# Gate products of the second up stage in the rounded format: the product split in a high and a low part, its low rows made on VectorE and ScalarE

## The chip, the core and the metric

The kernel runs on one core of a Trainium2 chip. TensorE (PE) multiplies, VectorE (DVE) and ScalarE (ACT) work on rows of 128 partitions, GpSimd (POOL) helps in a few stages, and SyncE (SP) issues the transfers. The metric is the device time of one execution in microseconds (us).

## The reference, cut to what matters

The program is two layers of a first kind of block, and then two layers of a second kind. The change touches the feed-forward part of the second kind, in which each of 256 tokens picks 128 of 16,384 experts (8 heads, 16 each). With `NK` = 128 keys a side, an expert is a pair (first key, second key).

```python
cand_i = top_i[:, :, 0, :, None] * PEER_NKEYS + top_i[:, :, 1, None, :]
best_s, best_j = lax.top_k(cand_s.reshape(c, PEER_HEADS, PEER_TOPK * PEER_TOPK), PEER_TOPK)
gate = jax.nn.softmax(best_s, axis=-1).astype(xc.dtype)
u = u_tab[idx]
act = jax.nn.gelu(jnp.einsum('chkd,cd->chk', u, xc), approximate=False)
vsel = v_tab[idx]
return jnp.einsum('chk,chkd->cd', gate * act, vsel)
```

The kernel does not gather. It computes gelu(u x) for all 16,384 experts, builds a dense table of gates (zero where an expert is not chosen), multiplies the two, and multiplies the result with all of v.

## The kernel before, in words

A product in which accuracy counts is made of three matmuls in the rounded 32-bit format (fp32r): each factor is split in a high part and the rest, and high*high, high*low and low*high are added in PSUM. ACT makes the high half of a weight piece (`split_hi`, line 182, `w_hi`), DVE the low half (`split_lo`, line 191, `w_lo`). A piece is 512 KB of raw weights in one of four slots; its two halves are two steps for each engine.

The feed-forward part of each layer of the second kind has three stages, each a block with a barrier at its end:

- **First up stage** (`choose_experts`): 64 tiles of 128 experts (one weight piece each) while DVE picks the experts. POOL makes half of the low parts here.
- **Second up stage** (`up_with_gates`): the other 64 tiles, in 16 rounds of `BODY` = 4. Beside them the gates are built (`GatePhase`).
- **Down stage** (`down_phase`).

In both up stages `UpPhase` does the tiles: 24 matmuls of 128x256 a tile (lines 224 to 226, `up_up`), then a gelu on ACT (line 2667, `expert_gelu`), then SP stores the tile's gelu to memory (line 2610, `expert_gelu_held`). Before the change `expert_gelu` has four buffers, so the gelu of tile j waits for the store of the tile four earlier.

In the second up stage, `GatePhase` works on `TOK` = 4 tokens a tile. `chosen` holds first keys, second keys and gates of all tokens, one token a column. DVE writes, for each of four tokens, a one-hot row of the first key times the gate (`first_keys`, line 2828, `onehot_first_gated`, `wgt`) and a one-hot of the second key (`second_keys`, line 2834, `onehot_second`, `one`). PE multiplies them, one fp32 matmul of 128x128x128 a token (`group`, line 2844, `gates_ps`); the profile shows each fp32 matmul as two weight loads and two matmuls. ACT moves the result to `gates` (`move`, line 2851). On PE the group of tile j-1 stands ahead of the up matmuls of tile j.

What SP does at the end of an up stage matters below. Inside the rounds it alternates: load the piece of tile j (which waits for the low half of the tile four earlier), then store the gelu of the tile four earlier. After the last round it issues four loads for the next stage, the last of which waits for the low halves of the last tile; then, in the second up stage, four fetches for the down stage (line 2613, `expert_back`); and only then the stores of the last four tiles.

Of the kernel before, what the change touches and what calls it, by code (L numbers as in the profile page):

```python
# [26 lines left out]
P = 128  # L27
# [4 lines left out]
L = 2  # L32
# [2553 lines left out]
def is_first(n):  # L2586
    return isinstance(n, int) and n == 0
# [9 lines left out]
class Shelf:  # L2597
# [9 lines left out]
        return piece(self.held, 0, NK, i)  # L2607

    def store(self, sp, j, i):
        sp.dma_start(self.place(i), self.out[:, j, :]).then_inc(self.stored[j], 16)  # L2610

    def fetch(self, sp, j, i):
        sp.dma_start(self.back[:, j, :], self.place(i)).then_inc(self.back_in[j], 16)
# [2 lines left out]
class UpPhase:  # L2616
# [41 lines left out]
    def scalar(self, act, gates=None, also={}, peel_last=0):  # L2658
        K, k0, shelf = self.K, self.k0, self.shelf

        def gelu(j, n):

            act.wait_ge(K.sem("w_used"), k0 + 2 * j + 2 + 2 * SLOTS * n)
            if self.which or not is_first(n):

                act.wait_ge(shelf.stored[j], 16 * (n + self.ROUNDS * self.which))
            K.nc.scalar.activation(shelf.out[:, j, :], self.up[:, j % 2, 0:SEQ], ACT.Gelu).then_inc(self.gelu_done, 1)  # L2667

        def body(n):
            for j in range(BODY):  # L2670
                for h in range(2):
                    K.split_hi(act, k0 + 2 * j + h, rep=n)
                if j > 0:
                    gelu(j - 1, n)
                elif not is_first(n):
                    gelu(BODY - 1, n - 1)
                if gates and j >= 2:
                    gates.move(act, j - 2, n)
                elif gates and not is_first(n):
                    gates.move(act, j + 2, n - 1)  # L2680
                if isinstance(n, int) and (n, j) in also:
                    also[n, j]()
        passes(act, body, self.ROUNDS, peel_first=1 if self.which else 2, peel_last=peel_last)
        gelu(BODY - 1, self.ROUNDS - 1)
        if gates:
            for j in (2, 3):
                gates.move(act, j, self.ROUNDS - 1)
# [112 lines left out]
class GatePhase:  # L2800
# [5 lines left out]

    def __init__(self, K, ctx, name, gates, iota, chosen):
        self.K, self.gates, self.iota, self.chosen = K, gates, iota, chosen
        self.one = K.sb("onehot_second", [P, 2, self.TOK, NK], F32, ctx)
        self.wgt = K.sb("onehot_first_gated", [P, 2, self.TOK, NK], F32, ctx)  # L2810
        self.ps = K.ps(f"{name}_ps", [P, BODY, self.TOK, NK], ctx)
        self.weighed, self.made, self.multiplied, self.moved = (
            K.sem(f"{name}_{s}") for s in ("weighed", "made", "multiplied", "moved"))

    def tokens(self, j, n, u=0, count=TOK):
        t = self.TOK
        if isinstance(n, int):
            return slice(t * (BODY * n + j) + u, t * (BODY * n + j) + u + count)
        return bass.ds(n * (BODY * t) + t * j + u, count)

    def first_keys(self, dve, j, n):

# [13 lines left out]

    def group(self, pe, j, n):
        pe.wait_ge(self.made, BODY * n + j + 1)
        pe.wait_ge(self.weighed, BODY * n + j + 1)
        if not is_first(n):  # L2840

            pe.wait_ge(self.moved, BODY * (n - 1) + j + 1)
        for u in range(self.TOK):
            ins = self.K.nc.tensor.matmul(self.ps[:, j, u, :], self.one[:, j % 2, u, :], self.wgt[:, j % 2, u, :],
                                          start=True, stop=True)
        ins.then_inc(self.multiplied, 1)

    def move(self, act, j, n):
# [6 lines left out]
def up_with_gates(K, phase, gates):  # L2855

    last = phase.ROUNDS - 1
    with K.nc.Block() as block:
        @block.sync
        def _(sp):  # L2860
            phase.sync(sp)

        @block.scalar
        def _(act):
            phase.scalar(act, gates)

        @block.gpsimd
        def _(pool):
            K.sweep(pool)

        @block.vector
        def _(dve):
            def body(n):
                for j in range(BODY):
                    phase.split_lo(dve, j, 0, n)
                    gates.first_keys(dve, j, n)
                    phase.split_lo(dve, j, 1, n)
                    gates.second_keys(dve, j, n)
            passes(dve, body, phase.ROUNDS)

        @block.tensor
        def _(pe):
            def body(n):
                for j in range(BODY):
                    if j > 0:
                        gates.group(pe, j - 1, n)
                    elif not is_first(n):
                        gates.group(pe, BODY - 1, n - 1)
                    phase.tensor_tile(pe, j, n)
            passes(pe, body, phase.ROUNDS)  # L2890
            gates.group(pe, BODY - 1, last)
    phase.end()
# [212 lines left out]
def second_layer(K, l, cols, table, after, entry, following):  # L3105
# [9 lines left out]
    ahead = lambda src: [(src(i), 512) for i in range(SLOTS)]  # L3115
    with ExitStack() as c0:
        chosen = K.sb("chosen", [P, 3, SEQ], F32, c0)
        gelu_out = K.sb("expert_gelu", [P, BODY, SEQ], F32, c0)
        gelu_back = K.sb("expert_back", [P, BODY, SEQ], F32, c0)
        with ExitStack() as cq:  # L3120
            with ExitStack() as c1:
# [210 lines left out]
def build(nc, ins, out):  # L3332
    with ExitStack() as ctx:
        K = Kernel(nc, ctx, ins, out)
        K.held = nc.dram_tensor("expert_gelu_held", [NK, P, SEQ], F32, kind="Internal").ap()
        K.cols1 = K.sb("p1_cols", [P, L, ins["cols1"].shape[2]], F32)
        K.cols2 = K.sb("p2_cols", [P, L, ins["cols2"].shape[2]], F32)
        table = K.sb("rotary_table", [P, 2, TT * M_HEADS, M_ROPE // 2], F32)
        in1 = [first_pieces(*first_weights(ins, l)) for l in range(L)]
        in2 = [second_pieces(ins, l)[:SLOTS] for l in range(L)]  # L3340
        first, later = K.sem("first_in"), K.sem("later_in")
        K.later_in = (later, 2 * 16)
        with ExitStack() as c1:
            rotary = RotaryTable(K, c1, table)
            with nc.Block() as block:
                @block.sync
                def _(sp):
                    rotary.sync(sp)
                    x = ins["x"].rearrange("b (t p) d -> p (b t) d", p=P)
                    for t in range(TT):  # L3350
                        sp.dma_start(K.x[:, t], x[:, t]).then_inc(first, 16)
                    sp.dma_start(K.ident[:], ins["ident"]).then_inc(first, 16)
                    sp.dma_start(K.cols1[:], ins["cols1"].rearrange("l p n -> p l n")).then_inc(first, 16)
                    K.prefetch(sp, in1[0])
                    for dst, src in ((K.cols2[:], ins["cols2"].rearrange("l p n -> p l n")), (K.iota[:], ins["iota"])):
                        sp.dma_start(dst, src).then_inc(later, 16)
                    sp.wait_ge(first, 4 * 16)

                @block.gpsimd
                def _(pool):  # L3360
                    for i, eps in enumerate((EPS1, EPS2)):
                        nc.gpsimd.memset(K.eps[:, i:i + 1], eps)

                @block.vector
                def _(dve):
                    rotary.vector(dve)

                @block.scalar
                def _(act):
                    rotary.scalar(act)  # L3370
        K.ahead = SLOTS
        K.open_banks()
        entry = RmsEntry(K, "norm1", K.cols1[:, 0, 0:DC], None, K.next_sem)
        entry.begin(K.half)
        for l in range(L):
            if l + 1 < L:
                following = lambda l=l: RmsEntry(K, "norm1", K.cols1[:, l + 1, 0:DC], by_token(K.left), K.next_sem)
            else:
                following = lambda: TurnEntry(K, "turn4", None, by_token(K.left), ROW2[0][1], K.next_sem)
            entry = first_layer(K, l, K.cols1[:, l], in1[l + 1] if l + 1 < L else in2[0], entry, following)  # L3380
        c0 = 6 + 2 * CF_K + 2
        ln2_gain, ln2_bias = (K.cols2[:, :, c0 + DC * i:c0 + DC * (i + 1)] for i in (3, 4))
        for l in range(L):
            if l + 1 < L:
                following = lambda l=l: LayerNormEntry(K, "ln2", ln2_gain[:, l], ln2_bias[:, l], by_token(K.left), ROW2[0][1],
                                                       K.next_sem)
            else:
                following = lambda: LayerNormEntry(K, "last", None, None, by_token(K.left), 512, K.sem)
            entry = second_layer(K, l, K.cols2[:, l], table, in2[l + 1] if l + 1 < L else [], entry, following)
# [19 lines left out]
```

## Time and profile before

| | us |
|---|---|
| median of 3 runs | 2756.87 (2755.52 to 2757.46) |
| the profiled execution, its own time | 2757.16 |
| its span, first to last instruction | 2755.4 |
| second up stage of the first such layer | about 1156.9 to 1402.5 |
| second up stage of the second such layer | about 2140.4 to 2385.9 |

How to read it: a row of the trace gives start, duration, engine, line, operation, output and inputs, and how many instructions it merges; in brackets stands the idle time before it and what ended it. PE rows are matmuls, PEld rows weight loads. Matmuls overlap, so their pace is the distance between two starts, not the duration of one. The profile merges neighbouring rows; of n equal instructions in a row of length T with duration d each, the pace is (T - d)/(n - 1).

### The profile page before, as it was taken

The page shows a single profiled execution, that of the slowest core. Times are in us where ns is not written, and L with a number is a line of the kernel's source. Part 1 is how long each engine was busy: PE and PEld are TensorE (multiplying, and loading weights), DVE is VectorE, ACT ScalarE, POOL GpSimd, SP SyncE. Part 2 cuts the span into 40 slices and gives each one's busy share as a digit, 9 for nine tenths or more (in the row PEclk, how much of TensorE's full clock was granted, in tenths as well). Part 3 has the DMA queues.
Part 4 walks back from the last instruction along what each step waited for, and adds up shares of the span by engine and source line. Part 5 has one row for each costly group of instructions (what it writes and reads, how often), then busy time and mean ns, then how long its engine had stood idle before and what let it go on. Part 6 is the DMA issues. An engine that isn't in the chain of part 4 may idle for free. (4 is left out here: it accounts for less than half of the span.)

```text
span 2755.4 us, 56513 instructions
## 1 busy us (share of the span) xinstructions
PE 2619.6 (95%) x17192; PEld 2372.9 (86%) x17192; DVE 2037.2 (74%) x4583; ACT 1498.2 (54%) x2973; POOL 220.8 (8%) x172
## 2 busy tenths in 40 slices
PE   7989999989988999999999999988999999999997
PEld 6769988779977899899988888777999999888886
DVE  5767767767768678877767777787689777677777
ACT  6555555655555455466655555555554566555554
POOL 0000000000000144300000000000344000000000
PEclk9999999999999999999999999999999999999999
DMA  5225654236653567655567777625676555677775
GB/s 202 85 69 178 187 160 161 77 115 183 184 173 106 163 213 228 184 177 174 175 199 242 239 240 243 222 86 177 186 227 205 173 174 174 183 241 240 243 240 183
DMA packets 194612, 503.52 MB, mean 183 GB/s; under 512 B 22608, under 2 KB 88400, under 8 KB 193104
## 3 DMA queue, kind: packets, MB, share of 16 engines
q1 hardware_dynamic: 194512, 502.28, 59.3%
q8 instruction: 52, 0.85, 0.1%
q14 instruction: 48, 0.39, 0.0%
HBM read 467.59 MB, written 34.60 MB: 182 GB/s over the span
## 5 line engine op out<-in xcount | busy, mean ns | idle before, releaser
L191 DVE TENSOR_TENSOR w_lo<-w_raw,w_hi 128x512 fp32r<-128x512 f32 (+1 forms) x1432 | 977.3, 686 | 362.0 <-ACT w_hi L182 340.9
L182 ACT ACTIVATE w_hi<-w_raw 128x512 fp32r<-128x512 f32 (+2 forms) x1592 | 926.8, 621 | 192.2 <-PE banks_right L226 138.0
L224 PE MATMUL up_up<-hT_hi,w_hi 128*128 128x256 f32 x2048 | 595.1, 291 | 9.6 <-DVE w_lo L191 8.8
L226 PE MATMUL up_up<-hT_hi,w_lo 128*128 128x256 f32 x2048 | 580.3, 283 | 0.0
L225 PE MATMUL up_up<-hT_lo,w_hi 128*128 128x256 f32 x2048 | 580.3, 283 | 0.0
L224 PEld LDWEIGHTS up_up<-hT_hi,w_hi 128*128 128x128 f32 x2048 | 393.4, 192 | 16.7 <-DVE w_lo L191 9.6
L236 PE MATMUL banks_left<-w_hi,expert_hi 128*128 128x512 f32 x1008 | 394.8, 392 | 8.1 <-DVE w_lo L191 8.1
L237 PE MATMUL banks_left<-w_lo,expert_hi 128*128 128x512 f32 x1008 | 394.2, 391 | 0.0
L238 PE MATMUL banks_left<-w_hi,expert_lo 128*128 128x512 f32 x1008 | 394.0, 391 | 0.0
L225 PEld LDWEIGHTS up_up<-hT_lo,w_hi 128*128 128x128 f32 x2048 | 393.8, 192 | 0.0
L226 PEld LDWEIGHTS up_up<-hT_hi,w_lo 128*128 128x128 f32 x2048 | 393.2, 192 | 0.0
L200 POOL TENSOR_TENSOR w_lo<-w_raw,w_hi 128x512 fp32r<-128x512 f32 (+1 forms) x160 | 212.6, 1329 | 1921.0 <-POOLq L2897 607.2
L224 PE MATMUL banks_right<-hT_hi,w_hi 128*128 128x256 f32 x1120 | 325.5, 291 | 8.2 <-DVE hT_lo L573 2.9
L225 PE MATMUL banks_right<-hT_lo,w_hi 128*128 128x256 f32 x1120 | 320.5, 286 | 0.0
L226 PE MATMUL banks_right<-hT_hi,w_lo 128*128 128x256 f32 x1120 | 320.5, 286 | 0.0
L2667 ACT ACTIVATE expert_gelu<-up_up 128x256 f32<-128x256 f32 x256 | 98.2, 384 | 385.3 <-PE up_up L226 385.3
L2746 ACT ACTIVATE expert_hi<-gates 128x256 fp32r (+1 forms) x256 | 106.9, 418 | 326.4 <-PE banks_left L238 323.4
L236 PEld LDWEIGHTS banks_left<-w_hi,expert_hi 128*128 128x128 f32 x1008 | 190.6, 189 | 48.1 <-DVE expert_lo L2762 8.4
L224 PEld LDWEIGHTS banks_right<-hT_hi,w_hi 128*128 128x128 f32 x1120 | 218.4, 195 | 14.8 <-issue 5.9
L238 PEld LDWEIGHTS banks_left<-w_hi,expert_lo 128*128 128x128 f32 x1008 | 190.5, 189 | 39.9
L237 PEld LDWEIGHTS banks_left<-w_lo,expert_hi 128*128 128x128 f32 x1008 | 190.7, 189 | 39.6
L2762 DVE TENSOR_TENSOR expert_lo<-gates,expert_hi 128x256 fp32r<-128x256 f32 x256 | 108.9, 425 | 156.7 <-ACT expert_hi L2746 156.7
(401 smaller groups left out, 3881.6 us busy)
## 6 DMA issues: line engine op xcount, KB each, us to landing
w_raw<-in_peer_u_c SPq DMA_DIRECT2D x256, 512.0 KB, 3.6
w_raw<-in_peer_v SPq DMA_DIRECT2D x256, 512.0 KB, 3.7
w_raw<-in_w_up_c SPq DMA_DIRECT2D x88, 512.0 KB, 3.7
expert_gelu_held<-expert_gelu SPq DMA_DIRECT2D x256, 128.0 KB, 1.7
expert_back<-expert_gelu_held SPq DMA_DIRECT2D x256, 128.0 KB, 3.4
w_raw<-in_w_down SPq DMA_DIRECT2D x44, 512.0 KB, 4.3
w_raw<-in_w_in_r SPq DMA_DIRECT2D x40, 512.0 KB, 3.7
w_raw<-in_w_in_c SPq DMA_DIRECT2D x32, 512.0 KB, 3.8
```

What stands on the lines that cost most here:

```text
L182: self.nc.scalar.activation(self.w_hi[:, k % SLOTS, 0:width], self.raw_half(k, width), ACT.Copy).then_inc(self.sem("w_hi_done"), 1)
L191: self.nc.vector.tensor_tensor(self.w_lo[:, k % SLOTS, 0:width], self.raw_half(k, width), self.w_hi[:, k % SLOTS, 0:width].bitcast(F32), A ...
L200: self.nc.gpsimd.tensor_tensor(self.w_lo[:, k % SLOTS, 0:width], self.raw_half(k, width), self.w_hi[:, k % SLOTS, 0:width].bitcast(F32), A ...
L224: self.nc.tensor.matmul(bank, hi, self.hT_hi[:, c, :], start=(c == 0), stop=False)
L225: self.nc.tensor.matmul(bank, hi, self.hT_lo[:, c, :], start=False, stop=False)
L226: last = self.nc.tensor.matmul(bank, lo, self.hT_hi[:, c, :], start=False, stop=(c == DC - 1))
L236: self.nc.tensor.matmul(bank, act_hi[:, cols], hi, start=start, stop=False)
L237: self.nc.tensor.matmul(bank, act_hi[:, cols], lo, start=False, stop=False)
L238: last = self.nc.tensor.matmul(bank, act_lo[:, cols], hi, start=False, stop=stop)
L2667: K.nc.scalar.activation(shelf.out[:, j, :], self.up[:, j % 2, 0:SEQ], ACT.Gelu).then_inc(self.gelu_done, 1)
L2746: K.nc.scalar.activation(self.hi[:, j % 2, :], tile_of(self.gates, j + BODY * n), ACT.Copy).then_inc(self.hi_done, 1)
L2762: self.K.nc.vector.tensor_tensor(self.lo[:, j % 2, :], tile_of(self.gates, j + BODY * n), self.hi[:, j % 2, :].bitcast(F32), ALU.subtract) ...
```

## The change

- `onehot_first_gated` and `onehot_second` are written in fp32r. So that no accuracy is lost, the gate is split in a high part (rounded to fp32r, which replaces it in `chosen`) and a low part; a new function, `split_gates`, makes the high parts and the ratio low/high (`gate_low_by_high`, `part`) for all 256 tokens ahead of the stage's first `split_lo`, in six DVE operations of 128x256 each, chained.
- Each tile has four more rows, `onehot_first_gated_low` = `onehot_first_gated` times that ratio: two on DVE (`first_low_too`), two on ACT (`first_low`). There is one buffer for them, so tile j's may be written when group j-1 is done on PE.
- The group has eight fp32r matmuls in place of four fp32 ones.
- To make room, `expert_gelu` gets two buffers in place of four, in both up stages: the gelu of tile j waits for the store of tile j-2 (for j of 2 and 3 that of the same round). A table of the first block is freed earlier, which changes addresses only.

```diff
     def store(self, sp, j, i):
-        sp.dma_start(self.place(i), self.out[:, j, :]).then_inc(self.stored[j], 16)
+        sp.dma_start(self.place(i), self.out[:, j % 2, :]).then_inc(self.stored[j], 16)
...
-            if self.which or not is_first(n):
-
-                act.wait_ge(shelf.stored[j], 16 * (n + self.ROUNDS * self.which))
-            K.nc.scalar.activation(shelf.out[:, j, :], self.up[:, j % 2, 0:SEQ], ACT.Gelu).then_inc(self.gelu_done, 1)
+            if j >= 2:
+                act.wait_ge(shelf.stored[j - 2], 16 * (n + 1 + self.ROUNDS * self.which))
+            elif self.which or not is_first(n):
+                act.wait_ge(shelf.stored[j + 2], 16 * (n + self.ROUNDS * self.which))
+            K.nc.scalar.activation(shelf.out[:, j % 2, :], self.up[:, j % 2, 0:SEQ], ACT.Gelu).then_inc(self.gelu_done, 1)
...
+    def split_gates(self, dve):
+
+        K, V, gate = self.K, self.K.nc.vector, self.chosen[:, 2, :]
+        link = lambda ins: K.dve.link(dve, ins)
+        low = self.low.rearrange("p u i -> p (u i)")
+        high, inverse = low[:, 0:SEQ], self.ps[:, 0, 0:2, :].rearrange("p u i -> p (u i)")
+        link(V.tensor_copy(high, gate))
+        link(V.tensor_tensor(self.part[:], gate, high.bitcast(F32), ALU.subtract))
+        link(V.tensor_copy(gate, high.bitcast(F32)))
+        link(V.tensor_scalar(inverse, gate, 1e-36, None, ALU.max))
+        link(V.reciprocal(inverse, inverse))
+        V.tensor_tensor(self.part[:], self.part[:], inverse, ALU.mult).then_inc(self.parted, 1)
+
+    def first_low(self, act, j, n):
+
+        act.wait_ge(self.weighed, BODY * n + j + 1)
+        if j >= 1 or not is_first(n):
+            act.wait_ge(self.multiplied, BODY * n + j)
+        for u in range(2, self.TOK):
+            ins = self.K.nc.scalar.activation(self.low[:, u, :], self.wgt[:, j % 2, u, :].bitcast(F32), ACT.Copy,
+                                              scale=self.part[:, self.tokens(j, n, u, 1)])
+        ins.then_inc(self.lowered_act, 1)
...
         pe.wait_ge(self.made, BODY * n + j + 1)
-        pe.wait_ge(self.weighed, BODY * n + j + 1)
+        pe.wait_ge(self.lowered_act, BODY * n + j + 1)
+        pe.wait_ge(self.lowered_dve, BODY * n + j + 1)
...
-            ins = self.K.nc.tensor.matmul(self.ps[:, j, u, :], self.one[:, j % 2, u, :], self.wgt[:, j % 2, u, :],
-                                          start=True, stop=True)
+            self.K.nc.tensor.matmul(self.ps[:, j, u, :], self.one[:, j % 2, u, :], self.wgt[:, j % 2, u, :],
+                                    start=True, stop=False)
+            ins = self.K.nc.tensor.matmul(self.ps[:, j, u, :], self.one[:, j % 2, u, :], self.low[:, u, :],
+                                          start=False, stop=True)
```

`first_low_too` is `first_low` for tokens 0 and 1, on DVE with `tensor_scalar`. It stands at the end of a tile on DVE; `first_low` stands at the end of a tile on ACT, behind `move`.

On DVE, at the start of the second up stage (`chosen` holds keys and gates, `w_lo` is a low half), it stood before:

```order
L3101 COPY chosen<-chosen_ps 128x256
L2980 UNCONDITIONAL_BRANCH
L2871 UNCONDITIONAL_BRANCH
L191 TENSOR_TENSOR w_lo<-w_raw,w_hi 128x512
L2828 TENSOR_SCALAR onehot_first_gated<-iota,chosen 128x128 x4
L191 TENSOR_TENSOR w_lo<-w_raw,w_hi 128x512
L2834 TENSOR_TENSOR onehot_second<-chosen,iota 128x512
```

and now:

```order
L2915 UNCONDITIONAL_BRANCH
L2835 CAST onehot_first_gated_low<-chosen 128x256
L2836 TENSOR_TENSOR gate_low_by_high<-chosen,onehot_first_gated_low 128x256
L2837 COPY chosen<-onehot_first_gated_low 128x256
L2838 TENSOR_SCALAR gates_ps<-chosen 128x256
L2839 RECIPROCAL gates_ps<-gates_ps 128x256
L2840 TENSOR_TENSOR gate_low_by_high<-gate_low_by_high,gates_ps 128x256
L191 TENSOR_TENSOR w_lo<-w_raw,w_hi 128x512
L2869 TENSOR_SCALAR onehot_first_gated<-iota,chosen 128x128 x4
L191 TENSOR_TENSOR w_lo<-w_raw,w_hi 128x512
L2875 TENSOR_TENSOR onehot_second<-chosen,iota 128x512
```

Six operations on 256 columns, one of them a reciprocal, stand ahead of the low half that PE's first matmul needs.

On PE, between the up matmuls of two tiles, before:

```order
L226 MATMUL up_up<-hT_hi,w_lo 128x256
L2844 MATMUL gates_ps<-onehot_first_gated,onehot_second 128x128 x4
L224 MATMUL up_up<-hT_hi,w_hi 128x256
```

and now:

```order
L226 MATMUL up_up<-hT_hi,w_lo 128x256
L2886 MATMUL gates_ps<-onehot_first_gated,onehot_second 128x128
L2888 MATMUL gates_ps<-onehot_first_gated_low,onehot_second 128x128
L2886 MATMUL gates_ps<-onehot_first_gated,onehot_second 128x128
L2888 MATMUL gates_ps<-onehot_first_gated_low,onehot_second 128x128
L2886 MATMUL gates_ps<-onehot_first_gated,onehot_second 128x128
L2888 MATMUL gates_ps<-onehot_first_gated_low,onehot_second 128x128
L2886 MATMUL gates_ps<-onehot_first_gated,onehot_second 128x128
L2888 MATMUL gates_ps<-onehot_first_gated_low,onehot_second 128x128
L224 MATMUL up_up<-hT_hi,w_hi 128x256
```

The place of the group is the same; it holds eight matmuls of the new format for four of the old.

## Rows read from the trace of the kernel before

**Rows 1.** The page: each engine's busy time, share of the span and instructions.
```profile
PE 2619.6 (95%) x17192; PEld 2372.9 (86%) x17192; DVE 2037.2 (74%) x4583; ACT 1498.2 (54%) x2973; POOL 220.8 (8%) x172
```

**Rows 2.** Stretch: busy PE, PEld, DVE, ACT, POOL; granted clock, DMA share, GB/s.
```profile
1200.00:1396.00 196.00, 196.00 (x1668) 196.00 (x1667) 152.07 (x366) 120.20 (x208) 0.00 (x0) 1.00 0.57 174
```

**Rows 3.** Timeline of PE, start and duration in us, one tile of the second up stage.
```profile
1253.10 0.28 PE L226 MATMUL up_up<-hT_hi,w_lo 128*128 128x256 f32 x1
1253.22 1.05 PE L2844 MATMUL gates_ps<-onehot_first_gated,onehot_second 128*128 128x128 f32 x8
...
1256.98 1.06 PE L2844 MATMUL gates_ps<-onehot_first_gated,onehot_second 128*128 128x128 f32 x8
```

**Rows 4.** Weight loads: timeline at 64 columns; durations (ns, min/median/max) of lines 1216 and 225.
```profile
127.30 0.97 PEld L1216 LDWEIGHTS banks_left<-row_products,att_probs_T 128*128 128x128 f32 x8
...
127.41 1.00 PE L1216 MATMUL banks_left<-row_products,att_probs_T 128*128 128x64 f32 x8
...
L1216 PEld LDWEIGHTS banks_left<-row_products,att_probs_T x160: 186/192/338, 127.3 to 563.2; 128*128 128x128 f32 x160
...
L225 PEld LDWEIGHTS up_up<-hT_lo,w_hi x2048: 187/192/338, 960.5 to 2383.2; 128*128 128x128 f32 x187
```

**Rows 5.** Timeline of PE in the down stage: fp32r matmuls of 512 columns.
```profile
1500.08 0.39 PE L236 MATMUL banks_left<-w_hi,expert_hi 128*128 128x512 f32 x1
1500.31 0.39 PE L237 MATMUL banks_left<-w_lo,expert_hi 128*128 128x512 f32 x1
```

**Rows 6.** Timeline of DVE, and of ACT, one tile of the second up stage.
```profile
1255.34 0.69 DVE L191 TENSOR_TENSOR w_lo<-w_raw,w_hi 128x512 fp32r<-128x512 f32 x1 [0.84 <-ACT w_hi L182]
1255.94 1.11 DVE L2828 TENSOR_SCALAR onehot_first_gated<-iota,chosen 128x128 f32<-128x128 f32 x4
...
1257.57 0.69 DVE L2834 TENSOR_TENSOR onehot_second<-chosen,iota 128x512 f32<-128x512 f32 x1
...
1260.95 0.38 ACT L2667 ACTIVATE expert_gelu<-up_up 128x256 f32<-128x256 f32 x1 [1.46 <-PE up_up L226]
```

**Rows 7.** Timeline at the start of the second up stage: ACT, DVE, PE.
```profile
1156.94 2.19 ACT L182 ACTIVATE w_hi<-w_raw 128x512 fp32r<-128x512 f32 x4 [0.84 <-PEq L2980]
...
1157.60 0.69 DVE L191 TENSOR_TENSOR w_lo<-w_raw,w_hi 128x512 fp32r<-128x512 f32 x1 [3.95 <-ACT w_hi L182]
...
1158.35 0.39 PE L224 MATMUL up_up<-hT_hi,w_hi 128*128 128x256 f32 x1 [2.67 <-DVE w_lo L191]
```

**Rows 8.** Groups by line and shape on DVE: a 256-column operation, reciprocals by width.
```profile
L2762 DVE TENSOR_TENSOR expert_lo<-gates,expert_hi 128x256 fp32r<-128x256 f32 x256 | 108.9, 425 | 156.7 <-ACT expert_hi L2746 156.7
...
L1516 DVE RECIPROCAL mean_squares<-root_mean_squares 128x32 f32<-128x32 f32 x2 | 0.7, 347 | 0.0
...
L3093 DVE RECIPROCAL gate_sums<-gate_sums 128x16 f32<-128x16 f32 x2 | 0.5, 252 | 0.1
```

**Rows 9.** End of the first up stage: ACT, SP, and the store issued at 1153.19.
```profile
1152.20 0.38 ACT L2667 ACTIVATE expert_gelu<-up_up 128x256 f32<-128x256 f32 x1 [2.23 <-PE up_up L226]
1155.72 0.38 ACT L2667 ACTIVATE expert_gelu<-up_up 128x256 f32<-128x256 f32 x1 [3.14 <-PE up_up L226]
...
1153.19 3.27 SPq L2610 DMA_DIRECT2D expert_gelu_held<-expert_gelu  x4
...
expert_gelu_held<-expert_gelu SPq DMA_DIRECT2D x1, 128.0 KB, 5.2
```

**Rows 10.** End of the second up stage: ACT, DVE, SP, the store issued at 1399.24.
```profile
1396.55 0.38 ACT L2667 ACTIVATE expert_gelu<-up_up 128x256 f32<-128x256 f32 x1 [1.45 <-PE up_up L226]
...
1400.60 1.88 ACT L2851 ACTIVATE gates<-gates_ps 128x512 f32<-128x512 f32 x2
...
1403.15 0.43 DVE L2757 TENSOR_TENSOR gates<-gates,expert_back 128x256 f32<-128x256 f32 x1 [5.61 <-PEq L2858]
...
1399.24 1.92 SPq L2610 DMA_DIRECT2D expert_gelu_held<-expert_gelu  x4
...
expert_gelu_held<-expert_gelu SPq DMA_DIRECT2D x1, 128.0 KB, 3.1
```

More of the change, by code:

```diff
@@ L2680, in body @@
                     gates.move(act, j + 2, n - 1)
+                if gates:
+                    if is_first(n) and j == 0:
+                        act.wait_ge(gates.parted, 1)
+                    gates.first_low(act, j, n)
                 if isinstance(n, int) and (n, j) in also:
@@ L2808, in __init__ @@
         self.K, self.gates, self.iota, self.chosen = K, gates, iota, chosen
-        self.one = K.sb("onehot_second", [P, 2, self.TOK, NK], F32, ctx)
-        self.wgt = K.sb("onehot_first_gated", [P, 2, self.TOK, NK], F32, ctx)
+        self.one = K.sb("onehot_second", [P, 2, self.TOK, NK], F32R, ctx)
+        self.wgt = K.sb("onehot_first_gated", [P, 2, self.TOK, NK], F32R, ctx)
+        self.low = K.sb("onehot_first_gated_low", [P, self.TOK, NK], F32R, ctx)
+        self.part = K.sb("gate_low_by_high", [P, SEQ], F32, ctx)
+        self.lowered_act, self.lowered_dve, self.parted = (K.sem(f"{name}_{s}") for s in ("lowered_act", "lowered_dve", "parted"))
         self.ps = K.ps(f"{name}_ps", [P, BODY, self.TOK, NK], ctx)
@@ L2819, in tokens, with first_low_too @@
         return bass.ds(n * (BODY * t) + t * j + u, count)
+    def split_gates(self, dve):
[17 more added lines that the diff above has]
+        ins.then_inc(self.lowered_act, 1)
+    def first_low_too(self, dve, j, n):
+        dve.wait_ge(self.weighed, BODY * n + j + 1)
+        if j >= 1 or not is_first(n):
+            dve.wait_ge(self.multiplied, BODY * n + j)
+        for u in range(2):
+            ins = self.K.nc.vector.tensor_scalar(self.low[:, u, :], self.wgt[:, j % 2, u, :].bitcast(F32),
+                                                 self.part[:, self.tokens(j, n, u, 1)], None, ALU.mult)
+        ins.then_inc(self.lowered_dve, 1)
     def first_keys(self, dve, j, n):
@@ L2872, in _ @@
         def _(dve):
+            gates.split_gates(dve)
             def body(n):
@@ L2875, in body @@
                     phase.split_lo(dve, j, 0, n)
+                    if is_first(n) and j == 0:
+                        dve.wait_ge(gates.parted, 1)
                     gates.first_keys(dve, j, n)
@@ L2878, in body @@
                     gates.second_keys(dve, j, n)
+                    gates.first_low_too(dve, j, n)
             passes(dve, body, phase.ROUNDS)
@@ L3117, in second_layer @@
         chosen = K.sb("chosen", [P, 3, SEQ], F32, c0)
-        gelu_out = K.sb("expert_gelu", [P, BODY, SEQ], F32, c0)
+        gelu_out = K.sb("expert_gelu", [P, 2, SEQ], F32, c0)
         gelu_back = K.sb("expert_back", [P, BODY, SEQ], F32, c0)
@@ L3335, in build @@
         K.held = nc.dram_tensor("expert_gelu_held", [NK, P, SEQ], F32, kind="Internal").ap()
-        K.cols1 = K.sb("p1_cols", [P, L, ins["cols1"].shape[2]], F32)
         K.cols2 = K.sb("p2_cols", [P, L, ins["cols2"].shape[2]], F32)
@@ L3340, in build @@
         in2 = [second_pieces(ins, l)[:SLOTS] for l in range(L)]
+        first_block = ExitStack()
+        K.cols1 = K.sb("p1_cols", [P, L, ins["cols1"].shape[2]], F32, first_block)
         first, later = K.sem("first_in"), K.sem("later_in")
@@ L3380, in build @@
             entry = first_layer(K, l, K.cols1[:, l], in1[l + 1] if l + 1 < L else in2[0], entry, following)
+        first_block.close()
         c0 = 6 + 2 * CF_K + 2
```

## The prediction

> **What bounds the kernel now.** I read the page first for the engines' shares: PE is busy 95% of the span, DVE 74%, ACT 54% [rows 1]. Then the busy times by stretch, for the stage that the change is in: from 1200 to 1396 us PE is busy in all 196 us at a granted clock of 1.00 (2.4 GHz), DVE in 152.07 and ACT in 120.20 [rows 2]. So the second up stage is PE's, and a tile there costs what PE takes. The timeline gives that: two groups of gate products start at 1253.22 and 1256.98, so a tile is 3.76 us [rows 3]. The up matmuls follow each other at 0.12 us (1253.10 to 1253.22 for the last of a tile), 24 of them are 2.88 us, and 0.88 us is left for the group: eight records of an fp32 product, 0.11 us each ((1.05 - 0.275)/7) [rows 3]. That 0.88 us, 128 times (64 tiles in each of two layers), is all that the change works on: 113 us.
>
> **The group in the new format.** Eight matmuls of 128 columns in fp32r replace eight records of fp32. An fp32r matmul of 256 columns has a pace of 0.12 us [rows 3], one of 512 columns 0.23 us [rows 5]: 107 and 213 ns at one column a cycle of 2.4 GHz, and some 13 ns more. By the stream alone 128 columns would take 53 + 13 = 66 ns. But a matmul also needs its weights loaded, and the trace has a place where the stream is too short to hide that: line 1216 multiplies 64 columns in fp32, two times 64 columns in a record or 53 ns, and its eight loads of 128x128 lie (0.97 - 0.19)/7 = 0.111 us apart [rows 4]. So a load of 128x128 four-byte weights has a floor of 0.11 us there, twice the stream. Whether fp32r weights load faster no row shows at a short stream; but a load is recorded with a median of 192 ns at line 1216 (fp32) and of 192 ns at line 225 (fp32r) [rows 4]. The nearest row for the load says that nothing changes, so I take 0.11 us a matmul: the group stays at 0.88 us, **0 us** gained. Bounds: 0.12 us a matmul, the pace that fp32r has at 256 columns, makes the group 0.96, +0.08 us a tile or +10 us; 66 ns makes it 0.53, -0.35 us a tile or -45 us.
>
> The Trainium skill (TensorE: Matmul & The Clock Gate, section LDWEIGHTS) gives the number of weight columns over 1.2 as a load's nanoseconds, 107 for 128 columns, and the row above, 0.111 us, agrees. The same page (section Weight-path perf modes) says that the fast weight load is used where the type is not FP32; it does not say on which side fp32r stands.
>
> **What DVE and ACT get.** A tile on DVE runs from 1255.34 to the end of `second_keys`, whose follower could start at 1257.57 + 0.60: 2.83 us of 3.76 [rows 6]. Two rows of 128 columns more, at the pace of `first_keys`, (1.11 - 0.34)/3 = 0.26 us, are 0.52: 3.35 us. ACT waited 1.46 us of a tile for PE [rows 6]; two operations of 128 columns cost it at most 0.38 us each, the duration of one of 256 columns: 0.76 us. Both fit, and both low rows are ready about a tile's up matmuls ahead of their group, since they wait only for the group before, which stands ahead of those matmuls. Cost **0 us**, hidden behind PE's 3.76 us as long as that stays above 3.35. Behind the new wait on ACT stand the next tile's two `split_hi`; they come some 0.6 us later, DVE's idle 0.84 us [rows 6] takes that up and PE has its low half still about 1 us early.
>
> **The split of the gates.** `split_gates` stands ahead of the low half that PE's first matmul waits for: DVE did that at 1157.60, PE started at 1158.35 [rows 7]. DVE could start when the block opens, with ACT at 1156.94. Five operations of 256 columns at 0.425 us are 2.1 us [rows 8]. The reciprocal grows with its width: 252 ns for 16 columns, 347 for 32, so 5.9 ns a column, and 256 columns are 0.35 + 224 x 0.0059 = 1.7 us [rows 8]. With some 0.04 us for each link, about 4.1 us; from 1156.94 that ends at 1161.0, against 1157.60: **+3.5 us a layer, 7 us** in all. PE has nothing else then. If the reciprocal were no dearer than the others, it would be +2.2 a layer.
>
> **Two gelu buffers at the end of a stage.** Inside the rounds the store of tile j-2 is issued right behind its gelu, and two tiles, 7.5 us, are more than its landing takes. At the end it is not so: the stores of the last four tiles stand behind SP's loads for the next stage. The gelu of the last but one tile now waits for the first of them.
>
> First up stage: that gelu ran at 1152.20; the store it will wait for is issued at 1153.19 and lands 5.2 us later, at 1158.4, with the load before it [rows 9]. Two of the four stores that shared the transfer now come later, so I take 4.6 us: 1157.8. The last gelu follows 0.3 us later, at 1158.1 against 1155.72: **+2.4 us**, and in the second layer by the same reckoning some 1.8 (its store landed after 4.2 us). Together **4.2 us** (3 to 6).
>
> Second up stage: the gelu ran at 1396.55; the store is issued at 1399.24 and lands after 3.1 us, at 1402.35 [rows 10]; DVE is some 0.6 us later with the last low half that the last load waits for, less contention takes some back: 1402.7. Behind that gelu on ACT stand a move (0.87 us), the two low rows of the last tile (0.6), for which PE's last group waits (0.9 and 0.2 until its result is seen), and then the last move (1.1): 1402.7 + 0.3 + 0.87 + 0.6 + 1.1 + 1.1 = 1406.7, against 1400.60 + 1.88 = 1402.48 [rows 10]. **+4.2 us, 8.4** in both layers (6 to 10). The block's barrier makes the down stage wait for it.
>
> **The sum.** 0 + 0 + 7.0 + 4.2 + 8.4 = +19.6 us. Against the profiled execution's own 2757.16 us that is 2776.8; the median is 0.3 us below it, so 2776.5. With the bounds of these terms, and the group at 0.88 to 0.96: 2768 to 2789.
>
> **Rivals.**
>
> 1. *The load of fp32r weights is short and the stream decides.* Group 0.53 us, PE's tile 3.41. DVE's 3.35 and its waits then stand right beside it, so perhaps 3.45: -0.31 x 128 = -40 us, with the ends +20: **2737**. For it: the eight loads need not behave as fp32's. Against: the recorded load durations are the same in both formats [rows 4]. A load floor between, 0.08 us, makes the group 0.64 and the sum -31 + 20 = -11: 2746. The Trainium skill (the same page, section Back-to-back issue gap) measured some 81 ns a matmul for a stream of loads and matmuls of 128 columns; by it the sum would be that 2746.
>
> 2. *The eight matmuls cost more than eight records.* Should an fp32r matmul this narrow be run as an fp32 one is, each would be two records, sixteen in a group at 0.11: 1.76 us, +0.88 x 128 = +113 us and the ends: **2890**. For it: no fp32r matmul under 256 columns is in the trace. Against: those of 256 columns are one record each.
>
> 3. *The last stores hide.* If the stage's end is not on the path (the down stage waits for something later anyway), 12.6 us of the sum are gone and 7 are left: 2764. Against: DVE's first step of the down stage came 0.7 us after the last move, ended by the block's barrier [rows 10].
>
> 4. *The group costs nothing more and DVE becomes late*: the low rows at 0.34 us each and every wait exposed make 3.5 us, still under 3.76; it decides only from a PE tile of 3.5 us on, so it belongs to rival 1, where it would bring 2737 up to 2744.
>
> **How the numbers follow.** Weight loads bound, ends exposed: 0.64, 2768 to 2789. Rival 1: 0.18, 2732 to 2750. Rival 2: 0.12, 2880 to 2900. Rival 3: 0.06, 2757 to 2768. To leave out no more than 2 in 10 the range takes in the first, rival 3 and most of rival 1, and leaves out rival 2: 2734 to 2790; the likeliest's own is 2768 to 2789. What a measurement of this kernel can tell from no change is about 0.2%, 5.5 us. Faster: rival 1, 0.16. Within: a little of rivals 1 and 3, 0.05. Slower: the rest, 0.79.
>
> **What would show it.** Starts of two groups 3.76 us apart in the middle of the stage, and the pace within one 0.11 (0.066 or 0.08 under rival 1, sixteen records under rival 2); DVE's idle in a tile down from 0.84 to about 0.3 and not gone; the reciprocal at 1.7 us and PE's first matmul of the stage 3.5 us after the place that it had; the last but one gelu of each up stage waiting for a transfer, and not for PE. The forecast is wrong above all if the group's pace is not 0.11.

## The result and the profile after

The changed kernel takes 2797.3 us (median of 4 runs, 2796.86 to 2797.74) against 2756.19 us beside it: a ratio of 1.0153, 95% interval 1.014 to 1.0165, or 41 us slower. The forecast was 2776.5, in a range of 2734 to 2790. The direction was right; the size, some 20 us, was half of what came.

First the place of the change. The timeline of PE in the middle of the second up stage, kernel after (start and duration in us, engine, line, operation):

```profile
1254.19 0.22 PE L2886 MATMUL gates_ps<-onehot_first_gated,onehot_second 128*128 128x128 f32 x1
1254.25 0.28 PE L2888 MATMUL gates_ps<-onehot_first_gated_low,onehot_second 128*128 128x128 f32 x1
1254.36 0.27 PE L2886 MATMUL gates_ps<-onehot_first_gated,onehot_second 128*128 128x128 f32 x1
1254.47 0.28 PE L2888 MATMUL gates_ps<-onehot_first_gated_low,onehot_second 128*128 128x128 f32 x1
...
1257.94 0.22 PE L2886 MATMUL gates_ps<-onehot_first_gated,onehot_second 128*128 128x128 f32 x1
```

A tile is 1257.94 - 1254.19 = 3.75 us, as it was (3.76, [rows 3]). The second, third and fourth matmul of a group start 0.11 us apart. So the group costs what it did. The stage by stretch, kernel after, in the columns of [rows 2]:

```profile
1200.00:1396.00 196.00, 196.00 (x1674) 196.00 (x1673) 172.96 (x470) 149.71 (x314) 0.00 (x0) 1.00 0.57 174
```

PE is still busy throughout; DVE has 173 us of 196 where it had 152, ACT 150 where it had 120, and neither delays PE. The 41 us are elsewhere. The first and the last up matmul of line 224 and the first and last matmul of the down stage in both traces give this account (us; the last column adds both layers):

| | first such layer, before | after | second layer, before | after | change, both |
|---|---|---|---|---|---|
| last up matmul of the first up stage to the first of the second | 3.19 | 8.26 | 3.18 | 8.32 | +10.2 |
| second up stage, first to last | 241.41 | 241.51 | 241.35 | 241.16 | -0.1 |
| last up matmul to the first of the down stage | 5.66 | 11.29 | 5.29 | 11.00 | +11.3 |
| down stage, first to last | 352.25 | 362.03 | 352.23 | 361.96 | +19.5 |

The two gaps cost 21.5 us more in the two layers together, where the prediction had 19.6. The last row it did not have at all, and the change has no line in the down stage. The gap between the up stages, kernel after: ACT, SP, DVE, PE.

```profile
1156.34 0.72 ACT L2668 ACTIVATE expert_gelu<-up_up 128x256 f32<-128x256 f32 x2 [7.34 <-DMA expert_gelu_held<-expert_gelu]
1158.04 1.15 ACT L182 ACTIVATE w_hi<-w_raw 128x512 fp32r<-128x512 f32 x2 [0.98 <-PEq L3029]
...
1152.23 5.33 SPq L2610 DMA_DIRECT2D expert_gelu_held<-expert_gelu  x4
...
1158.00 0.29 DVE L2835 CAST onehot_first_gated_low<-chosen 128x256 fp32r<-128x256 f32 x1 [5.30 <-PEq L3029]
...
1159.58 1.77 DVE L2839 RECIPROCAL gates_ps<-gates_ps 128x256 f32<-128x256 f32 x1
1161.38 0.42 DVE L2840 TENSOR_TENSOR gate_low_by_high<-gate_low_by_high,gates_ps 128x256 f32<-128x256 f32 x1
1161.72 0.69 DVE L191 TENSOR_TENSOR w_lo<-w_raw,w_hi 128x512 fp32r<-128x512 f32 x1
...
1162.46 0.58 PE L224 MATMUL up_up<-hT_hi,w_hi 128*128 128x256 f32 x1 [7.74 <-DVE w_lo L191]
```

Both last gelus stand together and wait for a transfer. The store issued at 1152.23 frees the first of them 4.1 us later, where the prediction took 4.6 [against rows 9]. The reciprocal is the 1.7 us worked out, and DVE's first low half comes 3.7 us after the block opens where it came 0.7 after [rows 7]. The other gap, ACT, SP and PE:

```profile
1407.83 0.38 ACT L2668 ACTIVATE expert_gelu<-up_up 128x256 f32<-128x256 f32 x1 [7.95 <-DMA expert_gelu_held<-expert_gelu]
1408.11 1.02 ACT L2895 ACTIVATE gates<-gates_ps 128x512 f32 x1
1408.92 0.66 ACT L2848 ACTIVATE onehot_first_gated_low<-onehot_first_gated,gate_low_by_high 128x128 fp32r<-128x128 f32 x2
1409.48 0.38 ACT L2668 ACTIVATE expert_gelu<-up_up 128x256 f32<-128x256 f32 x1
...
1411.67 1.02 ACT L2895 ACTIVATE gates<-gates_ps 128x512 f32<-128x512 f32 x1 [0.87 <-PE gates_ps L2888]
...
1404.02 6.21 SPq L2610 DMA_DIRECT2D expert_gelu_held<-expert_gelu  x4
...
1409.69 0.44 PE L2886 MATMUL gates_ps<-onehot_first_gated,onehot_second 128*128 128x128 f32 x1 [5.20 <-issue]
1409.93 0.42 PE L2888 MATMUL gates_ps<-onehot_first_gated_low,onehot_second 128*128 128x128 f32 x1
```

This is the chain of the prediction, in its order: gelu behind the store, move, low rows, last gelu and move, PE's last group, last move. Two things in it were not foreseen. The store issued at 1404.02 (0.6 us later than before, measured from the last up matmul, as reckoned) frees the gelu 3.8 us after its issue, where the prediction's 1402.7 left it 2.9: 0.9 us. And PE had idled over 5 us by then, and its last group runs at half the pace, 0.21 us a matmul, with the granted clock at 0.50, the lower level of 1.2 GHz: another 0.85 us. From the end of the last move to the down stage's first matmul it is 2.6 us, where it was 2.9; that gives 0.4 back.

Now the down stage. Timeline of PE, kernel after; [rows 5] has the same place of the kernel before:

```profile
1500.10 0.39 PE L238 MATMUL banks_left<-w_hi,expert_lo 128*128 128x512 f32 x1
1500.33 0.40 PE L236 MATMUL banks_left<-w_hi,expert_hi 128*128 128x512 f32 x1
1500.57 0.39 PE L237 MATMUL banks_left<-w_lo,expert_hi 128*128 128x512 f32 x1
```

The distances alternate between some 0.230 and 0.236 us, 233.3 ns in the mean, where those of before were 226 or 227 ns, 226.7 in the mean. PE waits for nothing and its clock is 1.00 in both. 1,536 matmuls a layer by 6.7 ns are 10.2 us (9.8 and 9.7 in the account). The pace is steady: every 20 us stretch of the first layer's stage from 1420 us on has a mean of 233.3 to 233.5 ns, so it is no disturbance that comes and goes. The loads are recorded at 188 ns before and 189 after, which tells nothing of it. What had changed for this stage is where its tiles lie. Two gelu buffers instead of four and the table freed early move everything behind them: in the built program `expert_hi`, the stationary operand here, stands at byte 217280 of a partition, and before at 220288. `w_hi`, the moving operand, stands at 57472 in both. Of these 3008 bytes, the gelu buffers are 2048 and the table is 960.

### The profile page after: what moved, and what is told of

The parts are those of the page before. It is cut to its first block and busy times, and to the rows that moved or that the text cites. A ratio compares the mean times of both kernels' runs of the same rounds, so it can differ in the third digit from the quotient of the medians.

```text
span 2795.7 us, 57903 instructions
## 1 busy us (share of the span) xinstructions
PE 2639.8 (94%) x17192; PEld 2375.5 (85%) x17192; DVE 2095.5 (75%) x4851; ACT 1569.0 (56%) x3229; POOL 220.9 (8%) x172
## 5 line engine op out<-in xcount | busy, mean ns | idle before, releaser
L236 PE MATMUL banks_left<-w_hi,expert_hi 128*128 128x512 f32 x1008 | 401.3, 398 | 7.3 <-DVE w_lo L191 7.3
L237 PE MATMUL banks_left<-w_lo,expert_hi 128*128 128x512 f32 x1008 | 401.0, 398 | 0.0
L238 PE MATMUL banks_left<-w_hi,expert_lo 128*128 128x512 f32 x1008 | 401.0, 398 | 0.0
```

The lines of the kernel that those rows point to most:

```text
L236: self.nc.tensor.matmul(bank, act_hi[:, cols], hi, start=start, stop=False)
L237: self.nc.tensor.matmul(bank, act_hi[:, cols], lo, start=False, stop=False)
L238: last = self.nc.tensor.matmul(bank, act_lo[:, cols], hi, start=False, stop=stop)
```

## Experiments: where the 20 us of the down stage come from

All kernels of one batch ran on the same chip with the kernel before. The measure besides the time is the number of PE matmuls in the stretch from 1420 to 1750 us, which lies in the down stage in all kernels of this section: 1,458 at 227 ns, 1,415 or 1,416 at 233 (1,451 in before_front64, where a wait of 1.5 us near the stage's end falls into the stretch).

**before_pad64.** The kernel before, one line more ahead of the loop over the last two layers:

```diff
+        K.sb("pad", [P, 16], F32)
```

> The kernel before with one unused tile of 64 bytes a partition ahead of the tiles of the last two layers, so that all of these stand 64 bytes higher; nothing else changes. Theory A (the 20 us that the sum lacked come from the address of the down stage's stationary tiles, which in the kernel after stand at 64 and in the kernel before at 0 past a multiple of 128 bytes): the down stage's matmuls go from 227 to 233 ns and the whole is +19 to +20 us, about 2776. Theory B (they come from the two gelu buffers, the later stores or another engine in the changed stages): no change, 2756.

Measured: 2774.06 against 2752.66 us, ratio 1.0085 (1.0068 to 1.0102). Nothing else of the change is in it, and 21 us are there, as many as were missing; in its trace the down stages are 10.0 and 8.7 us longer, and neither the second up stages nor the gaps are. Columns as in [rows 2]:

```profile
1420.00:1750.00 330.00, 330.00 (x1416) 265.90 (x1415) 241.67 (x472) 172.42 (x354) 0.00 (x0) 1.00 0.75 235
```

An unused tile of 64 bytes costs about what the prediction lacked. So theory B is out.

**after_pad64** and **after_pad_expert.** The same tile in the kernel after, first ahead of all tiles of these layers, then inside the down stage alone:

```diff
+        K.sb("pad", [P, 16], F32, ctx)
         self.hi, self.lo = (K.sb(f"expert_{x}", [P, 2, SEQ], F32R, ctx) for x in ("hi", "lo"))
```

> The kernel after with the same 64-byte tile, which brings these tiles back to a multiple of 128 bytes. Theory A: -19 to -20 us against the kernel after, so about 2778, +21 to +22 against before, which is what the ends of the stages cost. Theory B: 2797 as it was.

> The kernel after with the 64-byte tile inside the down stage alone, so that only expert_hi and expert_lo move (217280 to 217344), while gates, the fetched gelu and all tiles of other stages stay. If it is the stationary operand's address: about 2778, as with all tiles moved. If it is the address of gates or of another tile that DVE, ACT or a transfer uses beside the matmuls: 2797.

Measured: 2798.38 us (1.0165, 1.0148 to 1.0182) and 2795.27 us (1.0158, 1.0141 to 1.0175). Neither helped; both still have 1,415 or 1,416 matmuls in the stretch, 233.3 ns each. (In the second layer both run at a steady 232.4 ns, so the pace is not settled by the address to the last ns.) That a tile must stand at a multiple of 128 bytes, theory A as I had put it, is wrong: `expert_hi` stands at such a multiple in both (217344) and the pace is 233 ns. What the fast kernels had in common was another thing: 220288 and, in the next kernel, 218240 are both a multiple of 1024 above `w_hi`.

**before_gelu2.** The kernel before with two gelu buffers and the new waits, and nothing else of the change (the first two hunks of the diff, and the smaller tile).

> The kernel before with two gelu buffers in place of four and the new waits for the stores, nothing else of the change (expert_hi stays on a multiple of 128 bytes, 2048 bytes lower). By the prediction's step the ends of the first up stages cost about 2 us each; at the end of the second up stage there are no low rows behind the waiting gelu, so about 3.5 each: +11 us, 2767. If the ends hide: 2756. If the two buffers also slow the middle of a stage: more than 2770.

Measured: 2764.92 us, ratio 1.0044 (1.0027 to 1.0061), +12 us; the down stage at 227 ns. In its trace the gap between the up stages is 5.21 and 5.46 us (+2.0 and +2.3), that ahead of the down stage 8.84 and 8.70 (+3.2 and +3.4). The second up stages are 0.6 to 0.7 us longer and the down stages 1.2 shorter, which was not followed up. The step on the ends holds with its sizes: the prediction had +2.4 and +1.8, and the expectation some +3.5 for the second gap without low rows. And `expert_hi` stands 2048 bytes lower here without any harm, so what slowed the down stage in the kernel after is the table of 960 bytes, freed early.

**after_pad960** and **after_pad448.** The hunk of after_pad_expert with a tile of 240 or 112 columns, so that `expert_hi` stands 157 x 1024 bytes above `w_hi`, or 512 past a multiple of 1024.

> The kernel after with an unused tile of 960 bytes ahead of expert_hi in the down stage alone: expert_hi goes from 217280 to 218240, a multiple of 1024 bytes (157 x 1024) above w_hi at 57472, as the fast kernels before and before_gelu2 have it (159 and 157 x 1024). Theory C (the down stage's pace depends on where its stationary tile stands against its moving tile): matmuls back at 227 ns, -19.5 us, 2777 on the scale of before at 2756 (+21 against before). Theory D (the pace comes from the address of gates, the fetched gelu or another tile of the stage): 233 ns and 2797.

> As after_pad960, with 448 bytes: expert_hi stands 512 bytes past a multiple of 1024 above w_hi. 64 and 128 past were slow (233 ns). If the period is 512 bytes or a divisor of it above 128: 227 ns, +21 us against before. If it is 1024 or more: 233 ns, +41.

Measured: 2776.92 us (1.0082, 1.0065 to 1.0099) and 2778.18 us (1.0083, 1.0066 to 1.01). They are 22 and 24 us over before, where the kernel after was 41 over. The 960 bytes are just those of the freed table. The stretch in the down stage, in this order:

```profile
1420.00:1750.00 330.00, 330.00 (x1458) 273.25 (x1457) 248.65 (x485) 176.89 (x364) 0.00 (x0) 1.00 0.77 240
```

```profile
1420.00:1750.00 330.00, 330.00 (x1458) 273.25 (x1457) 248.71 (x486) 177.50 (x366) 0.00 (x0) 1.00 0.78 240
```

In both only `expert_hi` and `expert_lo` moved, so the addresses of gates, of the fetched gelus and of the other tiles by themselves are not it, though the expectation of after_pad_expert would have read its own result that way: its 64 bytes were only the wrong number.

**before_front64.** The 64 bytes ahead of all tiles of the program, so that all distances stay.

```diff
+        self.sb("pad", [P, 16], F32)
         self.x = self.sb("x", [P, TT, D], F32)
```

> The kernel before with the 64 bytes ahead of all tiles, so that all stand 64 bytes higher and their distances stay. If the distance of stationary and moving tile decides: 227 ns and no change, 2756. If the tiles' own place decides: 233 ns in the down stage and +20 us or more, since the up stages' tiles move too.

Measured: 2754.83 us (10 runs), ratio 1.0 (0.999 to 1.0009); the down stage's mean distance is 226.7 ns. Every tile stands 64 bytes off its former place and nothing is slower. `expert_hi` has the very address that it has in before_pad64, where it is slow. So it is not the address by itself but the distance of the stationary tiles from the tiles of the whole program, which the other shifts leave in place. PE reads one of those at the same time, the moving operand, and the table goes by it; but `w_lo` and the raw weights stand whole multiples of 512 bytes from `w_hi`, and no run tells them apart:

| kernel | `expert_hi` | distance to `w_hi`, past a multiple of 512 | matmul, ns |
|---|---|---|---|
| before | 220288 | 0 | 226.7 |
| before_gelu2, after_pad960 | 218240 | 0 | 226.7 |
| after_pad448 | 217728 | 0 | 226.7 |
| before_front64 | 220352 (`w_hi` 57536) | 0 | 226.7 |
| before_pad64 | 220352 | 64 | 233.3 |
| after | 217280 | 64 | 233.3 |
| after_pad64, after_pad_expert | 217344 | 128 | 233.3 (second layer 232.4) |

A distance of 256 past a multiple of 512 was not tried, so the period may be 256 or 512 bytes. Why the hardware does this the traces do not show.

## Experiments: what sets the price of a group

**before_high_only.** The kernel before with both one-hot tiles in fp32r, four matmuls a group, and the low part of the gates left out:

```diff
-        self.one = K.sb("onehot_second", [P, 2, self.TOK, NK], F32, ctx)
-        self.wgt = K.sb("onehot_first_gated", [P, 2, self.TOK, NK], F32, ctx)
+        self.one = K.sb("onehot_second", [P, 2, self.TOK, NK], F32R, ctx)
+        self.wgt = K.sb("onehot_first_gated", [P, 2, self.TOK, NK], F32R, ctx)
```

> The kernel before with both one-hot tiles in fp32r and four matmuls a group; the low part of the gates is left out, so the gates are rounded. It tells what sets the group. If the weight load does (0.11 us for each matmul): the group goes from 0.88 to 0.44 us, -0.44 x 128 = -56 us, 2700; DVE's 2.83 us stay under PE's 3.32. If the stream did (66 ns): 0.26, but DVE and ACT then come near, about -75 us.

Measured: 2702.9 us, ratio 0.981 (0.9793 to 0.9826), 52 us less, where the expectation by the load had 56.

```profile
1254.58 0.56 PE L2844 MATMUL gates_ps<-onehot_first_gated,onehot_second 128*128 128x128 f32 x4
1257.90 0.56 PE L2844 MATMUL gates_ps<-onehot_first_gated,onehot_second 128*128 128x128 f32 x4
```

A tile is 3.32 us: 2.88 and 0.44, four times 0.11. Half of the records, half of the price, and no sign of the 66 ns of the stream alone.

**after_bf16.** after_pad960 with the three one-hot tiles in bf16, still high and low, so a gate keeps about 16 bits:

```diff
-        self.one = K.sb("onehot_second", [P, 2, self.TOK, NK], F32R, ctx)
+        self.one = K.sb("onehot_second", [P, 2, self.TOK, NK], BF16, ctx)
...
-        self.low = K.sb("onehot_first_gated_low", [P, self.TOK, NK], F32R, ctx)
+        self.low = K.sb("onehot_first_gated_low", [P, self.TOK, NK], BF16, ctx)
```

> after_pad960 with the three one-hot tiles in bf16 in place of fp32r, still eight matmuls a group and high plus low. If the floor of 0.11 us is that of loading four-byte weights, two-byte ones load faster and the group falls to 8 x 0.06 to 0.08 = 0.5 to 0.65 us: -0.25 to -0.35 us a tile, as far as DVE's 3.35 us let it, -30 to -45 us against after_pad960, so 2732 to 2747. If any load of 128 columns takes 0.11 us: 2777 as after_pad960.

Measured: 2730.78 us, ratio 0.9911 (0.9894 to 0.9928), 24 us under before where after_pad960 was 22 over: 47 us gained, a little more than the 45 expected at most. Timeline of PE, then the loads of line 2888 (durations in ns, min/median/max), both of after_bf16:

```profile
1254.11 0.22 PE L2890 MATMUL gates_ps<-onehot_first_gated_low,onehot_second 128*128 128x128 bf16 x1
1254.16 0.22 PE L2888 MATMUL gates_ps<-onehot_first_gated,onehot_second 128*128 128x128 bf16 x1
1254.22 0.22 PE L2890 MATMUL gates_ps<-onehot_first_gated_low,onehot_second 128*128 128x128 bf16 x1
...
L2888 PEld LDWEIGHTS gates_ps<-onehot_first_gated,onehot_second x512: 95/98/152, 1166.2 to 2357.4; 128*128 128x128 bf16 x171
```

The same eight matmuls of 128 columns are 0.056 us apart, and a load is recorded at 98 ns. In the kernel after it was:

```profile
L2888 PEld LDWEIGHTS gates_ps<-onehot_first_gated_low,onehot_second x512: 187/192/339, 1167.8 to 2414.8; 128*128 128x128 f32 x171
```

For fp32 the load is shown to be the limit: the records of line 1216 are 112 ns apart both at 64 and at 96 columns, so the stream does not count there. For fp32r it is argued. The pace is the same 0.11 us, a load is recorded at 192 ns in both formats, and with two-byte tiles load and pace fall together. But after_bf16 made the moving operand narrower too; an fp32r stream that is slower at 128 columns than the 53 ns would give the same pace, and no run changes one operand alone. The Trainium skill (TensorE: Matmul & The Clock Gate, Weight-path perf modes) has the fast load for types that are not FP32; these rows, 192 ns a load against 98, put fp32r with FP32. The 81 ns a matmul that the same page (Back-to-back issue gap) gives for 128 columns is in neither: 111 ns here with four-byte weights, 56 with two-byte ones, and the measurement decides. The rival that rested on 66 ns was wrong for fp32r.

## Experiments: giving back what the ends cost

**after_turns.** after_pad960, and at the end of an up stage:

```diff
         for q, (src, width) in enumerate(self.next):
             K.load_piece(sp, k0 // 2 + HALF + q, src, width)
+            store(q, self.ROUNDS - 1)
...
-        for j in range(BODY):
-            store(j, self.ROUNDS - 1)
```

> As after_pad960, and at the end of an up stage SP stores the gelus of the last four tiles in turn with the loads for the next stage, as inside the rounds, in place of behind all loads and fetches. The last but one gelu then finds its store landed. Expected if the ends cost what the trace of after shows (the gap between the up stages +5.1 us of which the split is some 3.5 to 4, that ahead of the down stage +5.6): about -12 us against after_pad960, so +9 against before. If the low rows and the last group keep the end of the second up stage late whatever the stores do: only -4.

Measured: 2764.42 us, ratio 1.003 (1.0019 to 1.004), 12.5 us under after_pad960 and 8 to 10 over before, where +9 was expected. The last gelus wait for PE again:

```profile
1155.95 0.38 ACT L2667 ACTIVATE expert_gelu<-up_up 128x256 f32<-128x256 f32 x1 [3.14 <-PE up_up L226]
```

Its gap between the up stages is 6.21 us against 3.19, and that ahead of the down stage 5.93 against 5.66. What is left, 3 us a layer between the up stages, is the split of the gates.

**before_turns.** The same hunk in the kernel before, with its four buffers.

> The kernel before with the last four stores of an up stage in turn with the loads for the next. With four gelu buffers no gelu waits for them, so no change is expected, 2756 (bounds -4 to +2: the transfers at the stages' ends share the engines otherwise).

Measured: 2757.2 us, ratio 1.0007 (0.9997 to 1.0016): nothing clear of noise, as expected, though its trace has the gap ahead of the down stage 0.65 us longer in both layers (6.31 and 5.94). The order of the stores gains only where a gelu waits for them.

**bf16_four_gelu.** The change in bf16, with room for four gelu buffers; the stores in turn; and the split, one operation shorter, moved to the end of the first up stage, into DVE's wait for the block to end. A gate keeps about 16 bits here too. `expert_hi` stands 160 x 1024 bytes above `w_hi`.

```diff
+                to(V.tensor_copy(high[:], chosen[:, 2, :]))
+                to(V.tensor_tensor(ratio[:], chosen[:, 2, :], high[:], ALU.subtract))
+                to(V.tensor_scalar(inverse[:], high[:], 1e-36, None, ALU.max))
+                to(V.reciprocal(inverse[:], inverse[:]))
+                to(V.tensor_tensor(ratio[:], ratio[:], inverse[:], ALU.mult))
```

> The change in bf16, which takes so little room that all four gelu buffers stay; the low/high ratio is made at the end of the first up stage, where DVE waits 3.9 us for the block to end; the last stores in turn. The stages' ends should cost 0 to 1 us each, and the group gain what after_bf16 gains: 2710 to 2728. If the loads have the same floor in bf16: 2756 to 2760.

Measured: 2711.48 us, ratio 0.9837 (0.982 to 0.9853), 44 us faster than before, where the change was 41 slower. DVE at the turn of the stages, and one tile of the second up stage:

```profile
1153.90 1.75 DVE L3137 RECIPROCAL gate_high_inverse<-gate_high_inverse 128x256 f32<-128x256 f32 x1
1155.69 0.42 DVE L3138 TENSOR_TENSOR gate_low_by_high<-gate_low_by_high,gate_high_inverse 128x256 f32<-128x256 f32 x1
...
1157.35 0.69 DVE L192 TENSOR_TENSOR w_lo<-w_raw,w_hi 128x512 fp32r<-128x512 f32 x1 [1.24 <-ACT w_hi L183]
...
1254.55 0.68 DVE L192 TENSOR_TENSOR w_lo<-w_raw,w_hi 128x512 fp32r<-128x512 f32 x1
1255.15 0.68 DVE L2859 TENSOR_TENSOR onehot_second<-chosen,iota 128x512 bf16<-128x512 f32 x1
1255.76 0.41 DVE L2842 TENSOR_SCALAR onehot_first_gated_low<-onehot_first_gated,gate_low_by_high 128x128 bf16<-128x128 bf16 x2
```

The split nearly fits into the wait, not wholly: it ends at 1156.11, 0.9 us after the last gelu (1154.81 + 0.38), and the block ends behind it. The gap between the up stages is 3.85 us in both layers, where before had 3.19: 0.65 us a layer for the split in place of 3. The 1.24 us of idle time ahead of `w_lo` come after the block's end and are no room to spare. A tile is 3.38 us on PE, 217 us for the stage, and DVE is busy in 163.5 of 170 us (1200 to 1370): it has next to nothing left to give. Whether it already sets the tile was not tried.

## Why the prediction was wrong, step by step

- **The group in the new format: 0 us.** Right. The pace in a group is 0.11 us and the stage is unchanged (+0.1 and -0.2 us). The row of 64 columns [rows 4] told the size. That it is the load which sets it is shown for fp32 and argued for fp32r, as said above.
- **DVE and ACT hidden.** Right. DVE's idle ahead of a tile fell from 0.84 to 0.37 to 0.51 us (0.3 forecast), and PE never waits in the stage.
- **The split: +3.5 us a layer.** Mechanism right, size 3.0 to 3.1: the reciprocal took 1.77 us (1.7 worked out), but the two copies took 0.29 us each, not 0.425, and an operation began 0.03 us after the end of the one before it, not 0.04.
- **The ends of the first up stages: +2.4 and +1.8.** before_gelu2 has +2.0 and +2.3. Right, and 4.3 for 4.2 in the sum.
- **The ends of the second up stages: +4.2 each.** +5.6 and +5.7. Low by 1.4 to 1.5 us each: 0.9 is the landing of the store, 0.85 the last group at half the clock, and 0.4 came back behind it. The split, too dear by some 0.9 us in both layers, hid a part of it.
- **What the sum left out: the down stage, +19.5 us.** This is the step that failed. The prediction says that the 0.88 us of a group, 128 times, "is all that the change works on", and its sum has no term for the down stage; the description of the change says that the freed table "changes addresses only". I gave that no price and no bound. The prediction costed every instruction that the change touches, and took for granted that one whose line, operands and clock stay the same keeps its duration. Its address did not stay, and its matmuls went from 226.7 to 233.3 ns; before_pad64 shows that an address alone does this, after_pad960 that it goes when the 960 bytes are put back. With +19.5 the sum would have been 2796, against 2797.3 measured.
- **The rivals.** Rival 1 (66 or 80 ns a matmul) is out, since the pace is 0.11 us; rival 2 (sixteen records) is out, eight were recorded; rival 3 (ends hidden) is out by before_gelu2 and after_turns; rival 4 belonged to rival 1 and did not arise. None of them was the miss.
- **The bounds.** Those of the terms add up to 2770 to 2790, not 2768 to 2789. Nothing hangs on it: without the down stage's 19.5 us the time would lie inside either.

## What to carry to other kernels

Before a matmul is made cheaper by its type, ask which of its two parts is the longer: with a short moving operand the load of the stationary one can set the pace, and a group that trades four products of two records for eight of one gains nothing. When buffers shrink, look at the last rounds of the stage, where the queue that frees them has other work ahead. And when a change moves tiles, compare the addresses of the stationary and the moving operand in every stage behind it, not only in the stage that was edited.

## What the hardware showed that I had not expected

- An fp32r matmul of 512 columns took 226.7 ns where its stationary tile stood a multiple of 512 bytes from its moving tile, and 233.3 ns at 64 or 128 bytes past one (232.4 in the second layer at 128): 2.9%, 19.5 us over this kernel's 3,072 down-stage matmuls.
- Matmuls of 128 columns, each with a new load of 128x128 weights, were 0.11 us apart in fp32r, those of bf16 0.056 us; fp32 records were 0.11 us apart even at 64 columns.
- A reciprocal on DVE took 1.77 us for 256 columns, four times as long as a subtraction of the same shape (0.43 us).
